# Conditioning sums of a two-part transformer: from two engines and buffers of their own to VectorE and the weight ring

## What is computed

```python
def conv_gated_ffn(h, w_up, conv_w, conv_b, w_down):
    a = depthwise_conv_centred(h @ w_up, conv_w, conv_b)
    g, u = jnp.split(a, 2, axis=-1)
    return (jax.nn.silu(g) * u) @ w_down
...
# first block, for each of two layers:
x = x + mixed @ w_o[l]                      # mixed: attention and spatial gating of x @ w_in[l]
x = x + conv_gated_ffn(rms_norm(x, norm2_g[l]), w_up[l], conv_w[l], conv_b[l], w_down[l])
...
# second block:
mod   = (jax.nn.silu(c) @ w_ada[i] + b_ada[i])[:, None, :]
mod_c = jax.nn.silu(c_ctx) @ w_ada[i] + b_ada[i]
sh1, sc1, g1, sh2, sc2, g2 = jnp.split(mod, N_MOD, axis=-1)
csh1, csc1, cg1, csh2, csc2, cg2 = jnp.split(mod_c, N_MOD, axis=-1)
hc = rmsnorm(h_ctx, norm1_w[i]) * (1.0 + csc1) + csh1
```

## Time and profile before

| | |
|---|---|
| time, median of 3 runs | 4007.4 us (3997.7 to 4010.8) |
| profiled execution, span from its first to its last instruction | 4009.0 us |
| PE, DVE, ACT, POOL busy in it | 3717.9, 2477.5, 1747.8, 646.0 us |
| DMA, mean over the span | 171 GB/s |

### The profile page before, as it was taken

How to read it: one execution, slowest core, us unless ns; L and a number is a source line. 1 busy time by engine, 2 the same in 40 slices (tenths; PEclk the granted TensorE clock), 3 DMA queues, 4 the chain that set the end, 5 groups by cost and what they waited for, 6 DMA issues and landing times.

```text
span 4009.0 us, 44645 instructions
## 1 busy us (share of the span) xinstructions
PE 3717.9 (93%) x16234; PEld 2965.1 (74%) x16234; DVE 2477.5 (62%) x2262; ACT 1747.8 (44%) x1927; POOL 646.0 (16%) x379
## 2 busy tenths in 40 slices
PE   6989999998998989999998998999988889999998
PEld 5867777776777867777776777787753678888886
DVE  3655888988444654888888545236665555555454
ACT  4444565555433444655555433224421334333333
POOL 0001445453000001554444000000000000000000
PEclk9989999998999989999998999979988999999999
DMA  5535667665554534676666554235500345656564
GB/s 193 168 109 172 226 228 245 221 229 184 178 187 158 168 115 163 228 239 224 226 224 205 164 186 137 82 105 179 194 0 0 134 139 180 187 180 186 180 186 147
DMA packets 349116, 687.26 MB, mean 171 GB/s; under 512 B 15935, under 2 KB 20048, under 8 KB 347728
## 3 DMA queue, kind: packets, MB, share of 16 engines
q1 hardware_dynamic: 301136, 593.50, 44.7%
q10 hardware_dynamic: 47872, 92.29, 6.9%
HBM read 683.64 MB, written 2.10 MB: 171 GB/s over the span
## 4 chain that ended last, share of the span: by engine, by line
issue 47%; PE 24%; DVE 11%; DVEq 7%; POOLq 5%; DMA 3%; ACT 2%; ACTq 1%; POOL 1%; SPq 0%
POOLq L588 5%; DVE ada_sum L1105 4%; DVEq L1318 4%; PE acc L1994 3%; PE acc L1995 3%; PE acc L1996 3%; PE acc L1778 3%; PE acc L1780 3%; PE acc L1779 3%; DMA ada_raw<-in_w_ada 2%; DVE w_lo L1048 2%; DVEq L1295 2%; PE acc L2231 1%; PE side L2241 1%; DVE conv L1294 1%
## 5 line engine op out<-in xcount | busy, mean ns | idle before, releaser
L1048 DVE TENSOR_TENSOR w_lo<-w_raw,w_hi 128x2048 fp32r<-128x2048 f32 x362 | 816.2, 2258 | 568.1 <-ACT w_hi L621 567.5
L621 ACT ACTIVATE w_hi<-w_raw 128x2048 fp32r<-128x2048 f32 x362 | 678.6, 1879 | 569.8 <-DMA w_raw<-in_w_down 273.6
L1778 PE MATMUL acc<-w_hi,in_h 128*128 128x512 f32 x2112 | 866.0, 410 | 15.2 <-DVE in_l L1057 12.9
L1779 PE MATMUL acc<-w_lo,in_h 128*128 128x512 f32 x2112 | 855.2, 405 | 0.0
L1780 PE MATMUL acc<-w_hi,in_l 128*128 128x512 f32 x2112 | 854.0, 404 | 0.0
L587 POOL TENSOR_TENSOR ada_sum<-ada_sum,ada_term 128x512 f32<-128x512 f32 x330 | 553.4, 1677 | 393.0 <-ACT ada_term L793 351.7
L1105 DVE SCALAR_TENSOR_TENSOR ada_sum<-ada_raw,silu_c,ada_sum 128x512 f32<-128x512 f32 x330 | 487.6, 1478 | 36.0 <-issue 11.0
L1778 PEld LDWEIGHTS acc<-w_hi,in_h 128*128 128x128 f32 x2112 | 410.6, 194 | 116.2 <-issue 14.4
L1780 PEld LDWEIGHTS acc<-w_hi,in_l 128*128 128x128 f32 x2112 | 409.3, 194 | 101.2
L1779 PEld LDWEIGHTS acc<-w_lo,in_h 128*128 128x128 f32 x2112 | 410.6, 194 | 97.3
L1741 DVE TENSOR_TENSOR w_lo<-w_raw,w_hi 128x2048 fp32r<-128x2048 f32 x126 | 288.4, 2291 | 293.2 <-ACT w_hi L1024 293.2
(11 more groups left out here) (303 smaller groups left out, 4141.8 us busy)
## 6 DMA issues: line engine op xcount, KB each, us to landing
w_raw<-in_w_up SPq DMA_DIRECT2D x176, 1024.0 KB, 5.1
w_raw<-in_w_mlp SPq DMA_DIRECT2D x128, 1024.0 KB, 5.3
w_raw<-in_w_in SPq DMA_DIRECT2D x100, 1024.0 KB, 5.1
ada_raw<-in_w_ada ACTq DMA_DIRECT2D x176, 512.0 KB, 4.4
w_raw<-in_w_down SPq DMA_DIRECT2D x64, 1024.0 KB, 5.1
w_raw<-in_w_o SPq DMA_DIRECT2D x32, 1024.0 KB, 5.1
w_raw<-in_w_down SPq DMA_DIRECT2D x32, 768.0 KB, 4.5
w_raw<-in_w_out SPq DMA_DIRECT2D x16, 1024.0 KB, 5.1
```

Of the source, the lines that this page charges most:

```text
L621: nc.scalar.activation(hi[s][:, 0:n], raw[s][:, 0:n], ACT.Copy).then_inc(w_hi[s], 1)
L1048: nc.vector.tensor_tensor(lo[s][:, 0:n], raw[s][:, 0:n], hi[s][:, 0:n].bitcast(F32), ALU.subtract).then_inc(w_lo[s], 1)
L1778: nc.tensor.matmul(acc[p][i][:], ah_[:, kt, tok], hi[s][:, k], start=(kt == 0), stop=False)
L1779: nc.tensor.matmul(acc[p][i][:], ah_[:, kt, tok], lo[s][:, k], start=False, stop=False)
```

## The change

The second vector's sums leave ACT and POOL for DVE, and are made only for chunks 0 to 7. `ada_raw`, `ada_term`, `zero` and their semaphores go; POOL keeps only its small powers. The pieces of `w_ada` (four of 1 MB for a chunk) become positions of the weight ring, loaded by SP; DVE sums straight from `raw[s]` and frees the slot. The 22 chunks are spread anew: in the first layer's up stage pair 0 takes four pieces and the ten others two each, in its down stage c = 1 and 2 take four each; these are chunks 0 to 7, with two vectors. In the second layer all 11 pairs take four, and c = 1, 2, 3 of the down stage; chunks 8 to 21, with one vector. The loop over the two layers is written out in the program on all engines; the loop over pairs goes over two pairs at a time.

```diff
+    UP_ADA = ((4, 2), (4, 4))
+    UP_ORDER = {
+        2: ["p0", "p1", "p2", "a0", "p3", "p4", "p5", "p6", "a1", "p7"],
+        4: ["p0", "p1", "a0", "p2", "p3", "a1", "p4", "p5", "a2", "p6", "p7", "a3"],
+    }
+    DN_ADA = ((False, True, True, False), (False, True, True, True))
+    DN_ORDER = {
+        False: [f"p{i}" for i in range(12)],
+        True: ["p0", "p1", "a0", "p2", "p3", "p4", "a1", "p5", "p6", "p7", "a2", "p8", "p9", "p10", "a3", "p11"],
+    }
...
+        def ada_half(l, s, r, q, half):
+            for k in range(2 * half, 2 * half + 2):
+                dve.drain()
+                if k == 0:
+                    dve.wait_ge(w_loaded[s], r * 16)
+                for v in range(2 - l):
+                    c = silu_c[:, v, 4 * q + k:4 * q + k + 1]
...
+                        a = nc.vector.scalar_tensor_tensor(ada_sum[v][:], raw[s][:, k], c, ada_sum[v][:], ALU.mult, ALU.add)
+            if half == 1:
+                a.then_inc(w_hi[s], 1)
+                dve.drain().then_inc(w_lo[s], 1)
+                dve.sem_inc(w_free[s], 1)
+                if q == 3:
+                    dve.sem_inc(ada_sums, 1)
...
                 split_up(2)
                 if before is not None:
                     finish_pair(before)
+                if total is not None:
+                    modulate(l, total)
+                ada(0, 0)
                 split_up(3)
-                ada_piece(0)
+                ada(0, 1)
                 split_up(4)
-                ada_piece(1)
+                if na == 4:
+                    ada(1, 0)
                 split_up(5)
-                ada_piece(2)
+                if na == 4:
+                    ada(1, 1)
                 split_up(6)
-                ada_piece(3)
                 outer_taps(j, 0)
+                ada(na // 2, 0)
                 split_up(7)
-                ada_piece(4)
-                split_up(8)
-                ada_piece(5)
-                split_up(9)
-                ada_piece(6)
-                ada_piece(7)
+                ada(na // 2, 1)
+                if na == 4:
+                    split_up(8)
+                    ada(3, 0)
+                    split_up(9)
+                    ada(3, 1)
+                else:
+                    split_up(8)
+                    split_up(9)
...
                 for i in range(2, 14):
                     if i == 13:
+                        if DN_ADA[l][c]:
+                            modulate(l, ADA_DN[l] + sum(DN_ADA[l][:c]))
+                        add_to_x(r + DN_R[l][c + 1] - DN_R[l][c] - 1, 3, 1, c)
+                    split_down(c, i)
+                    if DN_ADA[l][c] and i in (2, 5, 8, 11):
+                        m = (i - 2) // 3
+                        pos = DN_ORDER[True].index(f"a{m}")
+                        for half in range(2):
+                            ada_half(l, pos % NS, r + pos // NS, m, half)
...
# PE, down stage
                 for i in range(12):
+                    down_product(1, c, i)
+                    if i == 10 and DN_ADA[l][c]:
+                        ada_total(l, ADA_DN[l] + sum(DN_ADA[l][:c]))
```

More of the change, by code:

```diff
@@ L90, in program @@
     band, at_band = sb("band_sb", [P, TT, TOK])
-    one, zero = sbt("one", [P, 1]), sbt("zero", [P, 1])
+    one = sbt("one", [P, 1])
     table, at_table = sb("table", [P, 408])
@@ L448, in _ @@
         sp.dma_start(ctx_first[:], t["ctx_2"][0].rearrange("(t p) d -> p t d", p=P)).then_inc(x_loaded, 16)
-        with sp.Fori(0, 2) as l:
+        for l in range(2):
             for b in range(2):
@@ L476, in _, with load_pair @@
                     piece(rows(w_o2, l * D + s * CH, 4, c * CH), s, rnd(l, R_O) + c)
[L477 to L484, removed]
+            def load_pair(j, _, rb, off, na, i, q0, __):
+                for pos, what in enumerate(UP_ORDER[na]):
+                    n, s, r = int(what[1]), (off + pos) % NS, rb + (off + pos) // NS
+                    if what[0] == "p":
+                        piece(rows(w_up2, l * D + n % 4 * CH, 4, j * CH + n // 4 * DFF), s, r)
+                    else:
+                        piece(rows(w_ada2, (q0 + n) * CH, 4, i * CH), s, r)
+            up_iterations(sp, l, load_pair)
+            for c in range(4):
+                ada = DN_ADA[l][c]
+                for pos, what in enumerate(DN_ORDER[ada]):
+                    n, s, r = int(what[1:]), pos % NS, rnd(l, R_DN[l] + DN_R[l][c]) + pos // NS
+                    if what[0] == "p":
+                        piece(rows(w_dn2, l * DFF + DN_AT[n] * P, DN_SIZES[n], c * CH), s, r, DN_SIZES[n])
+                    else:
+                        piece(rows(w_ada2, n * CH, 4, (ADA_DN[l] + sum(DN_ADA[l][:c])) * CH), s, r)
         sp.wait_ge(act_s, 2 * NPAIR + 1)
@@ L574, in root @@
             nc.gpsimd.tensor_tensor(dst, src, nhalf[:, 0:width], ALU.pow).then_inc(rstd, 1)
[L576 to L588, removed]
         nc.gpsimd.memset(nhalf[:], -0.5)
         nc.gpsimd.memset(one[:], 1.0)
-        nc.gpsimd.memset(zero[:], 0.0)
         pool.drain()
[L594 to L597, removed]
+        pool.sem_inc(one_s, 1)
+        for l in range(2):
+            s7 = l * 7
             root(s7 + 1, x_rstd[:], x_ss[:], TT)
@@ L663, in _ @@
                 square_sum(ctx_first[:, i, c * CH:(c + 1) * CH], c_parts[:, i, c:c + 1]).then_inc(x_sq, 1)
-        with act_.Fori(0, 2) as l:
+        for l in range(2):
             act_.wait_ge(t_full[0], unit(l, U_TAB)[1])
@@ L770, in centre, with up_pair, product_done @@
                                              scale=table[:, ds(at + (T_CW + 88), 1)], bias=table[:, ds(at + T_CB, 1)]).then_inc(conv_id, 1)
[L772 to L778, removed]
-                def split_up(n):
[L781 to L798, removed]
+            def up_pair(j, before, rb, off, na, i, q0, total):
+                tk = val(act_, l * (UL // 2) + j * 2 + (U_UP // 2 + 2))
+                def split_up(n):
+                    pos = off + up_piece(na, n)
+                    split_hi(pos % NS, rb + pos // NS)
+                def product_done(n):
+                    pos = off + up_piece(na, n)
+                    act_.wait_ge(w_free[pos % NS], rb + (pos // NS + 1))
                 split_up(2)
@@ L1781, in product, with ada_total @@
             last.then_inc(w_free[s], 1)
[L1783 removed]
+        def ada_total(l, i):
             pe.wait_ge(ada_mod, i + 1)
[L1786 to L1787 removed]
+            pe.wait_ge(ada_sums, i + 1)
+            n = 2 - l
             for f in range(4):
[L1789 to L1790 removed]
+                for c in range(n):
+                    last = nc.tensor.matmul(side[0][:, n * f + c:n * f + c + 1], ada_sum[c][:, f * P:(f + 1) * P], one[:], start=True, stop=True)
             last.then_inc(ada_post, 1)
```

205 lines of the change are left out of this document (103 added, 102 removed).

## The result

The changed kernel takes 4153.84 us (median; 4150.29 to 4157.26) beside 4009.1 us of the kernel before in the same runs (3997.7 to 4011.45): a ratio of 1.0368, interval 1.035 to 1.0386. It is slower by 145 us; the profiled spans, 4155.3 and 4009.0, differ by 146.3. The forecast was +170, 4177 us, with a range from 4105 to 4265.

A forecast was written before the change was run, and what follows sets the result against it. PE was taken to bound the kernel, with late ACT copies and slow DVE sums cutting into it in the up stages. Terms -38 + 160 + 48 = +170 us gave 4177 us, range 4105 to 4265.

The forecast's parts named there:

- The term that decides: Second layer's up stage: DVE waits 7.25 us for a just-freed slot's refill, four times a pair; 70.0 us against 55.3, +160 us.
- 41 + 4w: Second layer's pair in us: 41 of DVE's own work plus four waits of length w.
- The first layer's up stage: Pair 0 longer, pair 1 pays a last refill, later pairs 49 us with PE the bound; sum -38 us.
- the last refill in pair 1: First layer's up stage: pair 1 pays pair 0's last refill, of which PE's p0 and p1 cover all but 5 us.
- the 2.4 us of average for one-column sums and slow matmuls: First layer's up stage: added to PE's 46.6 us a pair for one-column sums, every second pair, and slower matmuls after; 49 us.
- The down stages: Stalls in chunks with sums and a wait at their end: about 14 us for two chunks, 6.5 for three; +48 us.
- 6 us, then 1.8 of one-column matmuls: End of a first-layer down chunk with sums: PE waits 6 us for a3's sums before its last product, then 1.8 us.
- With one vector it is 3 and 1: End of a second-layer down chunk with sums: PE waits 3 us, then 1 us of one-column matmuls.
- The stalls inside a chunk: Down stages, late splits and paired transfers: some 6 us in a first-layer chunk, 1.5 to 2 in the second layer.
- The refills did not hide: Rival: the four waits hide, faster at 3895 us, chance 0.06; the whole breaks even at a wait of 3.3 us.
- DVE's sums did not keep their price: Rival: 1.48 us a sum comes from something other than POOL, so DVE's sums stay dear; 4445 us, chance 0.04.
- The clock rival: Second layer: PE's clock stays low after idling, pairs of 86 us, 4350 us, chance 0.05; milder form, slow starts after gaps.

The follow-up runs named there:

- experiment 1: Changed kernel, DVE only: in pairs with four sum pieces each is summed whole at its own ring position, two splits and a sum piece before the refill's split; 3937.62 us.
- Experiment 3: Changed kernel with both halves of each sum piece one split earlier, so one split lies between a slot's release and its next content's split; 4055.91 us, ratio 1.0131.
- experiment 2: Changed kernel with the second layer's sums taking two of the four row tiles of a piece, all loads and waits kept; 4059.34 us, ratio 1.0145.
- Experiment 5: Changed kernel, PE only: in the down stages a chunk's one-column sums come after its last product instead of before it; 4123.03 us, ratio 1.0301.
- experiment 7: Kernel before, with 15 of 16 POOL additions cut from 512 to 8 columns, all else kept; 3869.94 us, ratio 0.9658.
- experiment 4: Kernel before, with sums on DVE alone and the second vector for 8 chunks; sum pieces keep their own two buffers and ACT's queue; 3918.32 us, ratio 0.9796.
- experiment 8: Changed kernel with ring-order sums, one-column sums after the last product, and own buffers on ACT's queue in the second layer's up stage; 3868.08 us, ratio 0.9659.

## Why the prediction was right

**The term that decides.** "DVE frees a0 with the second half, and its very next instruction is the split of p4": shown. The step took 7.25 us from the release to the split; the trace has 7.26 to 7.36 in the lines above and 7.4 in the mean of all 44, four a pair, each behind the second half of a sum piece. Pairs were to take 70.0 us and take 69.8. In nine pairs DVE's waits are 29.6 us of it and its own time 40.2, against 29.0 and 41.0: the mechanism is as forecast, and that the total fits to 0.2 us is luck, since two small errors cancel. Experiments 1 and 3 vary the distance, experiment 2 the work, and the pair follows each as 41 + 4w said, w being the length of a wait. By stage: pair 0 went from 55.7 to 67.8, +12.0 against 13; the nine others +132.8 against 132.3; the last, with the way into the down stage, +10.0 against 14.7. In all +154.8 against +160.

**The first layer's up stage** was right in sign and 17 us too cautious. Pair 0 was to cost 20 us more and costs 22.3 (76.1 against 53.8). Nine pairs give back 66.7 where the sum had 56.7 less 5 for the last refill in pair 1: they take 47.9 us, not 49 (each of the eight below 47.1 or 48.3, where 48 to 50 was the sign given). Two allowances were too large. The refill that was to reach pair 1 with 5 us reaches it with 1 (48.9), and the 2.4 us of average for one-column sums and slow matmuls are 1.1: the other eight pairs alternate between 47.1 and 48.3 us over PE's 46.6. The last pair with the way into the down stage gives 10.3 instead of 6.3. In that PE idles 5.06 us ahead of the first down product where it idled 9.43 before; I hadn't priced that.

**The down stages** came to +56 against +48, in range but made up otherwise. "6 us, then 1.8 of one-column matmuls" is the step that was too small: PE waits 7.42 and 7.79, then the sixteen records of one-column matmuls take 3.55, at a granted clock of 0.50 (1064.4 to 1068.0 us), the 1.2 GHz level. "With one vector it is 3 and 1": 4.45 to 5.33 and 1.4 to 1.8. The stalls inside a chunk were put too high in return: of 16.2 us for a first-layer chunk (32.5 / 2) 11.2 are the end, and 5 are left for the slow matmuls behind it, which I had in no term, and for the stalls, which I had at 6. Experiment 5 takes most of the wait away, and 20 us of the down stages with it. That +56 is close to +48 is in part luck: the end was too small and the stalls, as far as they can be told apart, too large.

**The rivals.** The refills did not hide, and break-even was put at a wait of 3.3 us. Experiment 3, with 5.0 in the mean, is still slower and experiment 1, with 1.0 to 2.6, is faster, so the sign does turn between them. DVE's sums did not keep their price: 750 ns in all 450, and experiment 7 gives the reason. The clock rival came in its mild form. The granted clock was 0.89 in the second up stage against 0.93, and a piece behind a gap begins slowly (timeline of PE, the changed kernel):

```profile
1713.72 0.70 PE L1814 MATMUL acc<-w_hi,in_h 128*128 128x512 f32 x1 [3.05 <-DVE w_lo L1050]
...
1717.20 0.43 PE L1816 MATMUL acc<-w_hi,in_l 128*128 128x512 f32 x1
1717.47 0.39 PE L1814 MATMUL acc<-w_hi,in_h 128*128 128x512 f32 x1
```

From 1713.72 to 1717.20 lie eight matmuls, 0.43 us apart instead of 0.234, the 1.2 GHz level (granted clock 0.52), and from there the 2.4 GHz level (0.99): some 1.6 us lost behind this gap. Behind longer gaps of the stage up to 14 matmuls in a row were slow, 2.7 us. The pair was bound by DVE, and so the loss lay inside PE's own idle time; 69.8 us leave it no room in the sum. In the down stages it was not covered, as said.

**Not foreseen, and open.** Of the 24 us between the forecast's +170 and the +146 of the spans, 17 are the first layer's up stage and 5 the second's, the down stages take 8 back, and 10 are in no term: the rest of the program is 9.5 us shorter in the changed kernel. That is the second block, which the change doesn't touch. It takes 1506 to 1511 us in the six experiments built from the changed kernel, 1522.2 in experiment 7 and 1536.9 in experiment 4, both built from the kernel before, the latter with the loop over layers written out on DVE. So it goes with the code that a kernel has and not with its times in the first block; what in the code does it is not shown. In experiment 4 two stretches of the MLP are 8 to 10 us longer each, one with a wait of ACT of 12.45 us for a transfer. No run was made to settle it.

## What to carry to other kernels

Where one in-order engine both frees a slot and needs the slot's next content, count the work between the two: it must cover the issue, the landing and every step before its own use, here 7.3 us, or the difference is paid each time and by all engines. Taking the ring's pieces in the order in which they come in gave that distance here. An engine at 54% can still set the time, so add its busy time and its waits along one period before calling it idle. And before work is moved off an engine for load's sake, look at the price of a neighbour's instruction with and without it, as the 1478 and 750 ns of the earlier trace rows.

## What the runs showed of the hardware

POOL's additions beside DVE's sums were worth 131.4 us of the up stages of the kernel before, though POOL was busy for only half of them (307.90 of 610 us in the earlier trace rows). The forecast priced their silence, with ACT's, at 63 us in the first layer and not by itself in the second, where the refills set the time; the expectation of experiment 7 had it right. The wait for a refill was constant to 0.1 us in the stretch shown (7.26 to 7.36), with the DMA at half load (share 0.52). At 1854.81 SP issued two transfers of 1 MB one behind the other; ACT began on the first 5.01 us later, no later than the 5.1 us to landing in the median. At a DMA share of 0.78 and 265 GB/s, experiment 8's, PE was still fed almost without gaps (busy for 398.80 of 400 us).
